# Six folds of the adaLN weights in other mixer slots, and two weight halves rounded ahead of the first chunk's copy

## The reference

```python
mod = (silu(c) @ w_ada[l] + b_ada[l]).reshape(B, 3, 3, D)      # shift, scale, gate of three sub-layers
y = sublayer(x * (1 + scale) + shift)
x = layer_norm(alpha * x + s * (1 + gate) * y)                 # s is 1/2 for the feed-forwards, 1 for the mixer
```

## Time and profile before

| what | us |
|---|---|
| median of 3 runs | 1308.52 (1307.3 to 1309.93) |
| profiled execution | 1309.4 |
| its span | 1307.7 |
| TensorE busy | 1269.9 (97%) |
| VectorE busy | 975.4 (75%) |
| ScalarE busy | 654.0 (50%) |
| GpSimd busy | 134.2 (10%) |

### The profile page before, as it was taken

One profiled execution on the slowest core, in us unless ns is written; L12 is line 12 of the kernel. 1 busy time (PEld: TensorE's weight loads), 2 busy tenths in 40 slices (PEclk: granted clock), 3 DMA queues, 4 the chain that ended last, 5 costly groups with the idle time before them and its releaser, 6 DMA issues.

```text
span 1307.7 us, 18638 instructions
## 1 busy us (share of the span) xinstructions
PE 1269.9 (97%) x7333; PEld 1052.9 (81%) x7333; DVE 975.4 (75%) x1263; ACT 654.0 (50%) x1024; POOL 134.2 (10%) x238
## 2 busy tenths in 40 slices
PE   6999999999999999999999999999999999999997
PEld 3788887998888778888888888889888787788886
DVE  3587866688868977888578888568787788776555
ACT  3544444668734554444354444367684355544440
POOL 4011001001101210000101000100001011000000
PEclk9999999999999999999999999999999999999999
DMA  9989874856566549888659888566755664886551
GB/s 326 311 290 298 289 259 117 290 178 210 168 187 219 201 146 320 274 277 287 226 185 315 287 279 287 162 222 198 227 160 179 206 223 154 256 288 193 185 189 61
DMA packets 199687, 298.42 MB, mean 228 GB/s; under 512 B 14704, under 2 KB 162736, under 8 KB 199600
## 3 DMA queue, kind: packets, MB, share of 16 engines
q1 hardware_dynamic: 178032, 220.58, 51.1%
q0 software_dynamic: 21568, 76.65, 18.7%
HBM read 296.12 MB, written 1.07 MB: 227 GB/s over the span
## 4 chain that ended last, share of the span: by engine, by line
PE 82%; DVE 8%; ACT 3%; issue 3%; SPq 2%; DMA 1%; POOL 1%; DVEq 0%; ACTq 0%; POOLq 0%
PE pg L1039 73%; DVE wlo L1711 2%; PE pt L1064 1%; SPq L286 1%; ACT whi L610 1%; DVE acc L1735 1%; DMA pro<-in_w_ada_dram 1%; DVE gates L2187 1%; ACT lnw L592 1%; PE pt L1440 1%; PE pt L1425 1%; DVE x L1834 1%; PE pt L1442 1%; DVE lnw L1831 1%; DVE gates L2176 1%
## 5 line engine op out<-in xcount | busy, mean ns | idle before, releaser
L1711 DVE TENSOR_TENSOR wlo<-wraw,whi 128x1024 fp32r<-128x1024 f32 (+1 forms) x408 | 479.9, 1201 | 158.0 <-ACT whi L610 157.7
L610 ACT ACTIVATE whi<-wraw 128x1024 fp32r<-128x1024 f32 (+1 forms) x408 | 406.9, 1036 | 176.6 <-PE pg L1039 103.2
L1039 PE MATMUL pg<-whi,hhi 128*128 128x512 f32 x1024 | 411.5, 402 | 6.2 <-DVE wlo L1711 2.1
L1039 PE MATMUL pg<-whi,hlo 128*128 128x512 f32 x1024 | 400.8, 391 | 0.0
L1039 PE MATMUL pg<-wlo,hhi 128*128 128x512 f32 x1024 | 400.7, 391 | 0.0
L1039 PEld LDWEIGHTS pg<-whi,hhi 128*128 128x128 f32 x1024 | 193.0, 188 | 52.7 <-DVE wlo L1711 8.3
L1039 PEld LDWEIGHTS pg<-whi,hlo 128*128 128x128 f32 x1024 | 193.1, 189 | 41.7
L1039 PEld LDWEIGHTS pg<-wlo,hhi 128*128 128x128 f32 x1024 | 193.4, 189 | 37.6 <-issue 0.5
L1735 DVE SCALAR_TENSOR_TENSOR acc<-aw,sc,acc 128x1024 f32<-128x1024 f32 x128 | 163.8, 1280 | 1.5 <-DMA aw<-in_w_ada_dram 1.3
L460 POOL DMA_DIRECT2D aw<-in_w_ada_dram x128 | 68.2, 533 | 754.3 <-DVE acc L1735 717.6
L1039 PE MATMUL pg<-whi,athi 128*128 128x512 f32 x352 | 138.2, 392 | 0.0
(11 more groups left out here) (327 smaller groups left out, 1277.7 us busy)
## 6 DMA issues: line engine op xcount, KB each, us to landing
wraw<-in_ffn_w_up_dram SPq DMA_DIRECT2D x176, 512.0 KB, 5.9
aw<-in_w_ada_dram POOLq DMA_DIRECT2D x128, 512.0 KB, 4.7
wraw<-in_w_in_dram SPq DMA_DIRECT2D x104, 512.0 KB, 4.9
wraw<-in_ffn_w_down_dram SPq DMA_DIRECT2D x88, 512.0 KB, 4.5
pro<-in_w_ada_dram SPq DMA_DIRECT2D x16, 512.0 KB, 9.8
wraw<-in_w_branch_dram SPq DMA_DIRECT2D x16, 512.0 KB, 5.2
wraw<-in_w_o_dram SPq DMA_DIRECT2D x16, 512.0 KB, 4.2
gatebc<-gate_dram POOLq DMA_DIRECT2D x6, 512.0 KB, 4.1
```

Of the source, the lines that this page charges most:

```text
L610: act.activation(hi_view(n)[:, 0:size], wraw[:, q, o:o + size], ACT.Copy).then_inc(S["w_hi"], 1)
L1039: ins = pe.matmul(out_ap, a[i], b[j], start=first and n == 0, stop=last and n == 2, skip_group_check=group)
L1711: dve.tensor_tensor(lo, a, hi_view(n)[:, 0:size].bitcast(F32), ALU.subtract).then_inc(S["w_lo"], 1)
```

## The change

Six of the 24 folds of the mixer's stage move. Those of slots 4, 6, 47, 51, 59 and 60 go; slots 3, 9 and 11 get one, and slots 44, 52 and 54 get a second one. A slot may now hold more than one fold. The count behind which GpSimd does `o_pow` goes from 24 to 25 loads, because all folds are now in slots up to 55. On ScalarE the copy of chunk 0 moves from the head of slot 4 to the end of slot 5, so that the splits of halves 7 and 8 stand ahead of it.

```diff
-    Q_ADA = [4, 6, 21, 22, 23, 24, 26, 27, 33, 38, 40, 42, 44, 46, 47, 48, 50, 51, 52, 53, 54, 55, 59, 60]
+    Q_ADA = [3, 9, 11, 21, 22, 23, 24, 26, 27, 33, 38, 40, 42, 44, 44, 46, 48, 50, 52, 52, 53, 54, 54, 55]
...
-    POOL_O = sum(q <= 55 for q in Q_ADA) + 2
+    POOL_O = ADA_N + 1
...
-                        if q in EV_Q and q != 36:
+                        if q in EV_Q and q not in (4, 36):
                             evac(EV_Q.index(q))
...
                         if 0 < q < SLOTS - 3:
                             split(2 * U_M + q + 3, 24 if (q + 3) // 2 in (2, 3) else 1024)
+                        if q == 5:
+                            evac(0)
...
-                        if q in Q_ADA:
+                        for n in range(Q_ADA.count(q)):
                             ada(g)
                             g += 1
```

## The result

The changed kernel is slower: median 1318.75 us (1314.79 to 1319.89, 4 runs) against 1309.03 (1307.3 to 1309.93, 4 runs) for the kernel before, ratio 1.0068 with a 95% interval of 1.0055 to 1.0081. By the ratio that is 8.9 us, three times the 2.8 forecast. The profiled execution has a span of 1318.1, 10.4 over before. In the code after, lines behind L900 have numbers two higher (`mm3` L1041, the subtraction L1713, the fold L1737, `gated` L2178).

A forecast was written before the change was run, and what follows sets the result against it. TensorE, busy 1269.9 of 1307.7 us, was taken to bound the kernel. Starts +0.7 and +0.4 and ends 2 x 0.85 gave +2.8, hence 1311.3 us predicted, range 1308.3 to 1315.0.

The forecast's parts named there:

- start, layer 0: First layer's mixer start: the third-chunk gain is spent on late `lg` and `ccol`; +0.7 us, between +0.3 and +0.9.
- end, layer 0: First layer's mixer end: VectorE 2.05 late at `o_gate(1)`, 1.20 given back at slot 60; 0.85 us lost.
- start, layer 1: Second layer's mixer start: `lg` in time, outcome resting on when half 12 lands; +0.4 us, between -0.3 and +0.9.
- end, layer 1: Second layer's mixer end: same as the first layer's, rows having the same distances; 0.85 us lost.
- half 12 could land up to 0.6 earlier: Mixer start: fold 0's load goes out sooner and fold 1's leaves the stretch, so half 12's weights may land earlier.
- fold 22's load, "I take 4.4": Second fold of slot 54: its load, issued at 417.9, takes 4.4 us, below the 5.0 median, landing at 422.3.
- fold 21's taken as in time: Mixer end, behind half 57: this fold runs from 419.75 to 421.0, with no wait for its load counted.
- Fold 20's wait: Slot 53: VectorE arrives at 414.5, the load takes 3.8 us and lands at 416.28, so it waits 1.8 us.
- Rival (B): Mixer end: contention with branch weights and first w_o unit makes loads 5.2 us; +4.4, 1312.9 us; chance with longer 0.21.
- the 0.75 before w_o: TensorE's wait before the output projection at 450.08, read as waiting for VectorE and expected to go.
- Fold 1 in slot 9: Mixer start: standing before `params()`, it delays everything behind by 1.20 us, holding `lg` to 252.3.
- Rival (C): Mixer end: loads of slots 53 to 55 hidden, -2.0 us or -3.9 with full start gains (1304.6); chance 0.07.

The follow-up runs named there:

- e1: Kernel before with only the copy of chunk 0 moved on ScalarE, all folds in their old slots; 1313.08 us, ratio to before 1.0025.
- e2: Kernel before with the copy moved and the start's folds changed (slots 3, 9, 11; none in 4, 6, 47); 1313.69 us, ratio to before 1.0033.
- e4: Changed kernel with its second fold in slot 6 in place of slot 9; 1316.51 us, ratio to before 1.0049.
- e8: Kernel before with three more VectorE operations ahead of the low part of half 13, layer 0 alone; 1315.90 us, ratio to before 1.0045.
- e3: Kernel before with only the end changed (second folds in 44, 52, 54; none in 51, 59, 60); 1314.12 us, ratio to before 1.0032.
- e5: Kernel before with the copy moved and folds 0 and 1 in slots 6 and 8 instead of 4 and 6; 1307.82 us, ratio 0.9985.
- e7: Kernel before with two more VectorE operations ahead of the low part of half 13, layer 0 alone; 1312.50 us, ratio to before 1.0019.
- e10: e1 with the one load that fold 0 releases cut to 128 of 1024 columns, both layers; 1307.74 us, ratio to before 0.9985.
- e9: Changed kernel with folds 0, 1 in slots 6, 8, second folds in 40, 42, slots 44 to 55 as before; 1305.40 us, ratio to before 0.9965.
- e11: e9 but with second folds in slots 40, 42, 44, 46 and none in 54, 55, 59, 60; 1303.00 us, ratio to before 0.9953.
- e6: e3 with the loads of folds 20 to 23 of both mixers cut from 1024 to 128 columns; 1307.03 us, ratio to before 0.9979.

## Why the prediction was wrong

The direction was right, and each fold that was said to wait for a load did wait. The time, 1311.3 with a range up to 1315.0, was too low. One profiled execution of each kernel, compared in the time at which TensorE ends a half, gives the sum by parts (the clock's share apart):

| part | forecast | waits | clock |
|---|---|---|---|
| start, layer 0 | +0.7 | +0.9 | +3.4 |
| end, layer 0 | +0.85 | +3.3 | +1.7 |
| start, layer 1 | +0.4 | +2.0 | 0 |
| end, layer 1 | +0.85 | +1.1 | -1.7 (before's own stretch at 1033.41) |

In this pair the waits are 7.3 and the clock 3.4. But the profiled execution of after is the slowest of its four. In the means over four runs each the difference is 9.2 (1318.0 less 1308.8), of which the clock has 3.8 to 4.7 (7.9 less the 3.2 to 4.1 of before on the chips of the experiments; after's four runs lie between 6.6 and 10.5). That leaves about 5 for the waits, against 2.8. So the clock is about half of the loss, and the table's waits are larger than after's usual ones.

- **A term that was put at nothing: TensorE's clock.** This is about half. The forecast added each wait at its own length. It never asked what TensorE does behind a wait, though before's own trace had the sign. TensorE, VectorE, ScalarE and GpSimd, then the clock, in two windows of before:

```profile
1032.00:1034.00 2.00, 1.73 (x10) 1.36 (x9) 2.00 (x3) 1.66 (x3) 0.00 (x0) 0.85 1.05 358
1034.00:1036.00 2.00, 2.00 (x6) 1.54 (x5) 2.00 (x4) 0.00 (x0) 0.00 (x0) 0.50 0.38 131
```

  The Trainium skill, TensorE: Matmul & The Clock Gate, section "What's actually happening", says that the array's clock falls to 1.2 GHz when the engine has been idle, and that the moment varies from run to run. The traces agree in the main. Behind the first 30 us the thirteen profiles have ten waits of TensorE of 2.0 us or more, and nine had a stretch at 0.50 with them: in the start of after, e1, e2, e4 and e8, in the end of after and e4, and in both ends of e3. The tenth, 2.39 in e4's second layer, had none. They also show what it leaves open: before's own stretch had no wait over 0.92 in front of it. e2, e5, e7 and e8 have one at the same place in layer 1 (from 1031.8 to 1038.6), and the other eight profiles have none there, so it comes and goes without the edit.
- **Failed step at the start: "half 12 could land up to 0.6 earlier".** It came 1.0 later, counted from the copy. The forecast saw that fold 0's load would go out early, and counted fold 1's, which leaves the stretch, as one load less in the way. It was not in the way before (1.59 MB in the table under e10), so there was nothing to win. And the early load goes ahead of half 12's in the same engines, which move 367 GB/s from 233 to 243 after and 377 before. e10 shows what that costs. The wait in `cumulated` was 2.30 instead of 1.3. Its net effect was hidden, since `rows` then had no wait left (+0.9 against +0.7). In layer 1 another half was late: half 10's weights came too late for `evac(1)`, and `small_T` waited 1.43. e4 and e9 had the same wait there (1.45, 1.36), e2, e5 and e11 had not, though e2 has after's start and e11 has e9's; what decides it is open.
- **Failed terms at the end: fold 22's load, "I take 4.4", and fold 21's taken as in time.** They measured 6.7 and 8.0. Fold 20's wait was right (1.61 against 1.8, its load 3.8), but fold 21 waited 2.08 where none was seen, fold 23 waited 1.85 where its load was to be 0.2 early, and chunk 13's wait was 3.74. Rival (B) named this mechanism, with 5.2 a load. It was right in kind, and the loads were longer still. The loads fell among the branch weights and the first of w_o. The Trainium skill, DMA: Bandwidth & Descriptors, section "SWDGE vs HWDGE vs iDMA", says that an engine takes turns between software and hardware queues. The trace is in keeping with it, with 3.8 for the load that was alone and 6.6 to 8.0 for the three that were not. The turns need not be equal in bytes, as the next section shows.
- **Right:** the gain of the moved copy at the third chunk (1.2 to 1.3 at the end of half 8 in layer 0); `o_pow` freed (VectorE waits 0.56 for it, 1.03 before); 1.2 given back behind slot 60 (10.4 late at half 59, 9.2 at half 64). The forecast read the 0.75 before w_o as a wait for VectorE, where the earlier trace rows has only `issue`; the runs bear it out, since the wait is there in every profile with folds in 59 and 60 and in none without. Fold 1 in slot 9, on which the forecast spent most of its words, was the small part: e2 less e1 is 0.6 us by the medians, within the noise.
- **The range.** Its own terms reach +7.8, 1316.3, and it was drawn at 1315.0; the median lies beyond both. Forecast and rivals all lacked the clock.
- **Rival (C)** was true of the fold order and false of the loads: e6, in which the loads are quick, gained 2.7 with the start as before, where (C) had 2.0.

## What to carry to other kernels

When an edit lets an engine run earlier, list the transfers that this engine releases and look at what they then go ahead of: here a copy moved for 1.2 us sent a load 3.5 to 4 us sooner, and that cost more than the copy won. Price a wait of TensorE at its length and then ask for the clock: with nine of the ten waits of 2.0 to 3.7 us came 3.41 or 6.83 us at half speed, which is 1.7 or 3.4 us more. Give prefetched work to slots where its engine is idle long before the critical chain, so that neither the work nor its load is met there: the other slots of e11 alone made a loss of 0.7% into a gain of 0.5%.

## What was not expected of the hardware

- TensorE's granted clock fell to 0.50 for 3.41 or 6.83 us with waits of 2.0 us and more, and the lost clock was 6 to 8 us per run in the kernels with such waits against 3 to 4 in those without (5.2 in e7, with a wait of 1.07).
- A load of 512 KB by GpSimd took 3.8 us alone, 8.6 (issued at 232.9, behind two more of 512 KB in its own queue and beside weight loads) and 8.0 (the longest of those issued from 416.6 on). One of only 64 KB took 6.4 in e10, behind the same two: there the time of a load is mostly its turn in the queues, not its own bytes, and yet its bytes are what the loads behind it pay for.
- Two busy queues did not share alike. From 235 to 238 after, with weight loads waiting, GpSimd's queue moved six times the bytes of SyncE's:

```profile
q0 software_dynamic: 244, 0.93, 89.3%
q1 hardware_dynamic: 159, 0.15, 14.6%
```

  From 421 to 424, among the branch weights, it was 0.40 MB against 0.68. SyncE's packets were 1.0 KB on average in the first stretch and 3.8 KB in the second, GpSimd's 3.8 and 3.7. Turns by packets would fit that; no experiment here tests it.
